# A diffusion layer on eight cores: hand-staged program against a dependency-graph list scheduler

## The reference, cut to what matters

```python
mod_x = split(silu(c) @ w_ada + b_ada, 6)            # also mod_c from c_ctx
hc = modulate(layer_norm(ctx), mod_c[0], mod_c[1]);  kc, vc = context_kv(hc, w_in)
h = modulate(layer_norm(x), mod_x[0], mod_x[1])
q, k, v, u, vb, ga, gb = split(h @ w_in)
ya = window_attention(rope(q), rope(k), v, kc, vc, sink)   # +-128 tokens, 256 context keys
yb = gelu(u) * (W_s @ layer_norm(gelu(vb)) * g + b)        # per 128-token chunk
mix = (sigmoid(ga) * (ya @ w_a) + sigmoid(gb) * (yb @ w_b)) @ w_o
x_mid = layer_norm(ALPHA * x + mod_x[2] * mix) * ln1_g + ln1_b
h2 = modulate(layer_norm(x_mid), mod_x[3], mod_x[4])
out = layer_norm(ALPHA * x_mid + mod_x[5] * ((silu(h2 @ w_g) * (h2 @ w_u)) @ w_out)) * ln2_g + ln2_b
```

## Time and profile before

| | us |
|---|---|
| three runs | 1183.34, 1185.09, 1185.57 |
| median | 1185.09 |
| profiled execution, span of its slowest core (first to last instruction) | 1181.4 |
| spans of the eight cores | 1174.1 to 1181.4 |
| PE busy in that span | 954.6 (81%) |
| DVE, ACT, POOL busy | 612.8, 393.1, 364.8 |
| share of the chain that ended last: PE, DVE, DMA, issue, ACT, POOL | 64%, 11%, 10%, 6%, 5%, 3% |

### The profile page before, as it was taken

One profiled execution on the slowest core, in us unless ns is written; L12 is line 12 of the kernel. 1 busy time (PEld: TensorE's weight loads), 2 busy tenths in 40 slices (PEclk: granted clock), 3 DMA queues, 4 the chain that ended last, 5 costly groups with the idle time before them and its releaser, 6 DMA issues.

```text
span 1181.4 us, 16880 instructions; the slowest of 8 cores (1174.1 to 1181.4 us)
## 1 busy us (share of the span) xinstructions
PE 954.6 (81%) x5317; PEld 451.6 (38%) x5317; DVE 612.8 (52%) x1191; ACT 393.1 (33%) x744; POOL 364.8 (31%) x280
## 2 busy tenths in 40 slices
PE   0235799968888999997771399999999999989970
PEld 0122355524444444443331244444444444424420
DVE  0386441844644222223897116666666666674773
ACT  0297133256663222221489811111111111101542
POOL 2000451568974222222645050110111011010565
PEclk9999899967668999999995599999999999999995
DMA  9993846011113994006974180320330222020477
GB/s 185 170 246 89 171 83 108 10 46 54 55 28 48 151 167 107 1 1 149 225 177 90 50 222 16 72 43 30 72 72 2 71 72 37 1 36 1 70 106 110
DMA packets 33206, 101.73 MB, mean 86 GB/s; under 512 B 3168, under 2 KB 3296, under 8 KB 31200
## 3 DMA queue, kind: packets, MB, share of 16 engines
q0 software_dynamic: 22384, 51.32, 27.1%
q1 hardware_dynamic: 10736, 49.33, 14.3%
HBM read 118.40 MB, written 16.78 MB: 114 GB/s over the span
## 4 chain that ended last, share of the span: by engine, by line
PE 64%; DVE 11%; DMA 10%; issue 6%; ACT 5%; POOL 3%; DVEq 0%; SPq 0%; ACTq 0%; POOLq 0%
PE bank L1209 11%; PE bank L1205 11%; PE bank L1240 11%; PE bank L939 5%; PE bank L943 5%; PE bank L810 4%; DMA arena<-wada 3%; DMA arena<-xh 3%; PE bank L834 3%; PE bank L536 3%; PE bank L592 2%; PE bank L951 2%; PE bank L947 2%; DMA arena<-wff 2%; ACT arena L1113 2%
## 5 line engine op out<-in xcount | busy, mean ns | idle before, releaser
L1250 DVE TENSOR_TENSOR arena<-bank,arena 128x512 f32<-128x512 f32 x288 | 191.4, 685 | 26.6 <-DVE arena L1250 22.0
L1240 PE MATMUL bank<-arena 128*128 128x512 bf16 x704 | 169.8, 381 | 10.4 <-DVE arena L1250 10.4
L1212 ACT ACTIVATE arena<-bank 128x512 f32<-128x512 f32 x88 | 52.3, 597 | 369.3 <-PE bank L1205 362.5
L1205 PE MATMUL bank<-arena 128*128 128x512 bf16 x704 | 168.0, 382 | 6.9 <-ACT arena L1113 4.7
L1209 PE MATMUL bank<-arena 128*128 128x512 bf16 x704 | 166.6, 379 | 0.3 <-DVE arena L1215 0.3
L1215 DVE TENSOR_TENSOR arena<-bank,arena 128x512 bf16<-128x512 f32 x88 | 60.6, 691 | 168.7 <-PE bank L1209 163.2
L1240 PEld LDWEIGHTS bank<-arena 128*128 128x128 bf16 x704 | 66.5, 98 | 102.6 <-issue 29.9
L1205 PEld LDWEIGHTS bank<-arena 128*128 128x128 bf16 x704 | 69.0, 98 | 91.4 <-issue 9.8
L242 POOL DMA_DIRECT2D arena<-wff x11 | 8.7, 794 | 300.4 <-PE bank L1240 299.7
L1209 PEld LDWEIGHTS bank<-arena 128*128 128x128 bf16 x704 | 69.0, 98 | 84.1 <-issue 2.0
L813 ACT ACTIVATE arena<-bank 128x512 bf16<-128x512 f32 x160 | 80.0, 648 | 34.6 <-PE bank L810 34.6
(11 more groups left out here) (120 smaller groups left out, 1283.1 us busy)
## 6 DMA issues: line engine op xcount, KB each, us to landing
...
out<-ln2b SPq DMA_DIRECT2D x16, 512.0 KB, 25.8
...
```

The source lines that it names most:

```text
L1205: t_g_ = S.op('pe', lambda e, k=k, pg=pg, slot=slot, fi=fi, tok=tok: e.matmul(pg, lhsT=w1[slot][:, k, fi * 128:(fi + 1) * 128], rhs=h2T[:, ...
L1212: t_s = S.op('act', lambda e, dst=sgb[s_], pg=pg: e.activation(out=dst, in_=pg, func=AF.Silu), deps=[t_g_, sg_free[s_]])
L1240: t_mm = S.op('pe', lambda e, pd=pd, fi=fi, t=t, half=half, ab=ab, slot=slot, i_mm=i_mm, n_mm=n_mm: e.matmul(pd, lhsT=ab[:, fi, t * 128:(t ...
L1250: t_ad = S.op('dve', lambda e, accv=accv, pd=pd: e.tensor_tensor(out=accv, in0=pd, in1=accv, op=ALU.add), deps=[t_mm, t_acc[t]])
```

## The change

The program is written again. Operations are recorded in a `Graph` whose dependencies come from the bytes that each operand touches; `schedule` then fixes each engine's order by list scheduling: among the operations that are ready by its own cost table the one that was written first. No barrier is left; the order is static and each engine still runs it in sequence. Buffers share SBUF regions by overlap of addresses, which the dependencies see. The diff, cut to its core (the new side; of the old side the lines quoted by number above go):

```diff
+    def cost(self, eng, name, a, kw, out, ins):
+        if name in ('dma_start',):
+            return (1.0 if eng == 'pool' else 0.07)
...
+    def schedule(self):
...
+            p, i = heapq.heappop(avail[e])
...
+            if o.dma:
+                s = max(end + 0.8, pipe[0])
+                pipe[0] = s + o.bytes / 300e3
+                done = pipe[0] + 1.8
...
+    def stats(src, n, st, mv):
...
+        G.op('dve', lambda e: e.bn_aggr(out=mv[:, 0:2], in_=st[:, 0:6 * (n // 512)]))
+        G.op('dve', lambda e: e.tensor_scalar(out=mv[:, 2:3], in0=mv[:, 1:2], scalar1=EPS, scalar2=None, op0=ALU.add))
+        G.op('pool', lambda e: e.tensor_tensor(out=mv[:, 8:9], in0=mv[:, 2:3], in1=neghalf[:, 0:1], op=ALU.pow))
+        G.op('dve', lambda e: e.scalar_tensor_tensor(out=mv[:, 9:10], in0=mv[:, 0:1], scalar=-1.0, in1=mv[:, 8:9],
...
+    def a1_norm(n):
...
+        G.op('pool', lambda e: e.tensor_scalar(out=dst, in0=src, scalar1=rstd, scalar2=nmr, op0=ALU.mult, op1=ALU.add))
...
+    def a1_evac(n, b0, eng2):
...
+            pt = bkb(b0 + c // 4)[:, (c % 4) * 256:(c % 4 + 1) * 256]
...
+    for i, h in enumerate((0, 1, 4, 5, 2, 3, 6, 7)):
+        cast_load(flat(wada0[i]), wada_d[h])
+        col_block(h, wada0[i], 0 if i < 4 else 1)
...
+    for g in range(4):
+        if g < 3:
+            a1_pair(2 * g + 3, 6, 'act')
+            a1_pair(2 * g + 4, 6, 'act')
+        else:
+            a1_pair(9, 6, 'act')
+        k_unit(g)
+        for m in range(4):
+            q_unit(m, g)
+            u_unit(m, g)
+        for t in range(4 * g, 4 * g + 4):
+            v_unit(t)
+            vb_unit(t)
...
+    def att(j):
...
+            G.op('act', lambda e, s=s, b0=b0: e.activation(out=flat(P[:, s]), in_=bk(b0, 2), func=AF.Exp, scale=0.125))
+            if s in (0, 2):
...
+                G.op('dve', lambda e, s=s, mi=mi: e.tensor_tensor(
+                    out=P[:, s], in0=P[:, s], in1=masks[:, mi:mi + 1, :].to_broadcast([128, 8, 128]), op=ALU.mult))
...
+            G.op('act', lambda e, x=x, pg=pg: e.activation(out=t2[:, x], in_=pg, func=AF.Tanh, scale=0.5))
...
+        if (j - 4) % 3 != 2 and c1_i[0] < 8:
+            m = c1_i[0]
+            c1_unit(m, 0, (6, 7, 6, 7))
...
+    for t in range(NT):
+        G.op('sp', lambda e, t=t: e.dma_start(out=out_d[t * 128:(t + 1) * 128, :], in_=ln2b_d))
...
+        G.op('dve', lambda e: e.scalar_tensor_tensor(out=w, in0=x, scalar=ALPHA, in1=bk(2, 2), op0=ALU.mult, op1=ALU.add))
...
+    for t in range(4):
+        c2(t)
+    for m in range(8):
+        for g in range(1, 4):
+            bs = ((0, 1, 6, 7), (6, 7, 0, 1))[g % 2]
+            c1_unit(8 + m, g, bs)
...
+    for t in range(4, NT):
+        c2(t)
...
+            G.op('dve', lambda e: e.tensor_tensor(out=acc, in0=bk(b0, 2), in1=acc, op=ALU.add))
```

More of the change, by code:

```diff
@@ new lines, in build_nc @@
+    gvb = [at(kb(110 + 2 * i), F32, 512) for i in range(4)]
+    xnb = [at(kb(134 + 2 * i), BF16, D) for i in range(2)]
+    scb = at(kb(138), BF16, 8, 128)
+    wst = at(kb(140), BF16, 8, 128)
+    wada0 = [at(kb(62 + 4 * i), BF16, 8, 256) for i in range(4)] + [at(kb(118 + 4 * i), BF16, 8, 256) for i in range(4)]
+    wqk = at(kb(142), BF16, 8, 640)
+    wvvb = at(kb(152), BF16, 8, 640)
+    wu = at(kb(162), BF16, 8, 512)
+    hcT = at(kb(170), BF16, 8, CTX)
+    ropec = at(kb(174), F32, TH)
+    ropes = at(kb(183), F32, TH)
@@ new lines, in build_nc @@
+    a1_pair(0, 4, 'dve')
+    a1_pair(1, 6, 'dve')
+    cast_load(flat(wqk), wqk_d)
+    load(ropec, ropec_d)
+    load(ropes, ropes_d)
+    a1_pair(2, 2, 'dve')
+    cast_load(flat(wvvb), wvvb_d)
+    cast_load(perm, perm_d)
+    cast_load(flat(wu), wu_d)
+    cast_load(flat(masks), masks_d)
+    cast_load(flat(wst), wst_d)
+    load(esink, esink_d)
+    load(glgc, glgc_d)
+    load(flat(bias2), bsbc_d)
+    G.op('pool', lambda e: e.memset(vaug[:, :, :, 64:66], 1.0))
+    G.op('pool', lambda e: e.memset(vcaug[:, :, :, 64:66], 1.0))
@@ L1359, in finish @@
+                tail(t)
+    G.emit(nc, es)
     es.close()
+    nc._graph = G
     return nc
```

1968 lines of the change are left out of this document (793 added, 1175 removed).

## The result

1131.49 us (median of four runs, 1129.51 to 1134.71) beside 1184.21 for the kernel before on the same chip: a ratio of 0.956, 95% interval 0.9537 to 0.9583. Faster, as forecast, but by 53 us where 105 were forecast.

What follows compares the result with a forecast made beforehand. PE was taken to bound C1 and the FFN at the upper clock, leaving savings at seams and in C2. Stage terms summed to 1076.5 us, plus 3.7 for the median: 1080, range 1050 to 1110 (wide range 1020 to 1150).

Steps and rivals of the forecast that it cites:

- rival 3: Attention: PE stays at the lower clock throughout, 219 us instead of 138, total 1160; chance 0.13.
- Start, 119: Up to the first projection: transfers on SP's and POOL's queues add, copies into out included; taken as 119 us.
- rival 1: Start: the copies hide in the gaps of the other queue, start 85, 34 us less, total 1046; chance 0.15.
- rival 2: Start: copies starve POOL's queue, so modulation weights, wvvb and wu come late, 22 us more, total 1102; chance 0.17.
- Attention, 138: Attention with a quarter of C1: PE's work of 86, 41 and 11 us sets it, 138 us, to 378.
- Rival 4: DVE's [128x1] instructions around norms are held by POOL, at worst 364 us; total 1190, slower; chance 0.06.
- Exp and tanh: Attention: their 21 changes on ACT add nothing; with a table load at each, up to 27 us more, total 1107.
- Rest of C1, 145: C1 after attention: 24 units, four C2 tiles' w_o products and bank changes take 145 us, to 523.
- C2, 80: C2's remaining 12 tiles: DVE's pace of 5.4 us each, plus 4 at the start and 11 at the end, 80 us.
- FFN, 435.5: FFN: 2,016 matmuls at 0.216 us make 435.5, with the 17.25 us weight transfer at its start gone.
- Tail, 38: After PE's last matmul: 30 us as before plus 8 for POOL's powers on the last eight tiles, 38 us.
- Rival 5: Whole kernel: a static order made with 300 GB/s leaves PE waiting for late operands; no size or chance of its own.

## Why the prediction was right and wrong

The median, 1131.5, is 51 us above the forecast of 1080 and outside 1050 to 1110, but inside the wide range of 1020 to 1150. That is in part luck: above 1110 the range stood for half of rival 3, which did not come about, and the two waits that took the time, in attention and at C2's end, were in no sum.

- **Start, 119: right in size, and by the term that was disputed.** The copies cost 48.9 us and nothing of them hides; rival 1 (85 with them in place) is out, and 85 was still too high for a start without them (72.2). But the way to it was partly wrong, and the fit within 2.1 us is partly luck: the transfers that the sum had at 112 were there at 106, and the 7 us behind them took 15. The modulation slices on POOL's queue came last (106.2 us with the copies, 57.7 without), 1.3 us behind tile 6 on SP's. That is rival 2's mechanism, whose 22 us I had put on top of the sum. The copies ended later on both queues, and the first projection only once, by 48.9 us; wqk, wvvb and wu landed at 118, 132 and 138, and the projections got no longer for it. The Trainium skill (DMA: Bandwidth & Descriptors, Queues, rings and completion order) has engines go round their queues packet by packet, and slices that end 48.5 us later beside copies on another queue agree with it; how long a packet is, no run shows.
- **Projections, 121: right** (120.2).
- **Attention, 138: the step that failed first.** It counted PE's work and put its waiting at nothing. The work took 124.7 us, some of it at the lower clock, 13 less than the 138; 34.6 us of idle time came on top. Of the two ways in which DVE or ACT could set it, neither did by its total: masks left out, 26 us less on DVE, left attention's length as it was (the run without masks); exps in the old form gave nothing. What was shown to cost is DVE's products held beside POOL's multiplications, 10.0 us of PE's waits and 11.6 by the run without them, and PE's waiting as such: 96 matmuls, 20.7 us of work, fit in for 8.4. Rival 4 was right in kind, at 11.6 us instead of 105, and in another place than I looked: on wide products (32 mask products with 0.93 us in the mean, 0.68 alone), while the [128x1] rows stay at a median of 0.15; in C2 their mean is 0.41 and the worst 2.16. Rival 3 is out: the clock was 0.88, not 0.67, and rose to 0.94 when PE was given more.
- **Exp and tanh: right to add nothing.** The changed kernel has five table loads; with sigmoid there are 21 more, the number that the text had counted, and they cost 19 us of the 27 that it set as the limit. The Trainium skill (ScalarE: Activation LUTs, Table sets: the hidden batching unit) has the pair in one set, and these loads agree.
- **Rest of C1, 145: right** (146.9).
- **C2, 80: the second that failed.** The pace was 6.4 us a tile, not 5.4: 70 us for 11 steps where 65 stood for 12, and uneven: 5.2 us where PE and DVE take turns, 8.0 to 9.4 in four steps. The last tile's way took 30 us, not 11. The 11 left out POOL's multiplication, the accumulating transfer and the queues on POOL and ACT that the order puts before them. Three ways of making a tile's chain shorter left the time where it was: the last tile took 20 to 27 us then, but a slower pace (6.9 and 7.1 us with more work on DVE) or late FFN weights (without ln1_g) used it up. The loss is PE's 29 us of idle time: half of it at an end where the order had no more FFN work open, where 56 matmuls more and a better clock behind them gave back 13.2, and half in the steps before it, eleven of which took 67 to 72 us here and in the runs with late copies, without the gate and with more matmuls open.
- **FFN, 435.5: PE's 436.7 us are right**, the 8.7 more are idle time and clock at the two ends, as the windows show: a granted clock of 0.60 at first, behind C2's idle end, and PE busy 32.4 of 36.2 us while the last norms take DVE. The "3.45" that PE was said to need for a tile with its share of gate and up is 16 matmuls; it is 12, 2.59 us, and DVE's 1.28 lies below that too.

```profile
652.30:662.00 9.70, 8.01 (x26) 2.94 (x26) 2.44 (x2) 4.35 (x9) 6.21 (x3) 0.60 0.55 167
...
1060.00:1096.20 36.20, 32.35 (x146) 14.09 (x148) 29.11 (x60) 12.09 (x12) 25.95 (x21) 1.00 0.66 113
```

- **Tail, 38: 34.0**; six multiplications and not eight tiles were left to POOL behind PE's last matmul. Its power took about the 0.96 of the sum there: 0.91 us in the mean of twelve in the last 70 us (0.64 over all 84).
- **Rival 5, a static order that waits**, is what C2's end and the run without ln1_g show: SiLUs and FFN matmuls stand in a fixed order ahead of a tile's norm and wait for weights or tokens. It was priced nowhere; in C2 it is part of the 30 us of the last tile, and how much of them is the order alone was not tried.

What stays open: what each cause of C2's long steps is worth, and why attention waits for ACT and DVE in turn beyond the 10.0 us that are held products. PE's idle time there was filled, not taken apart.
